# Rotary halves exchanged by ScalarE copies instead of permutation matmuls, in a six-stage transformer kernel

## The chip, the cores and the metric

One core of one Trainium2 chip. The metric is the device time of one execution of the whole program, in microseconds (us); the time of a kernel is the median of its executions. Engines are named TensorE (PE; PEld is its weight load), VectorE (DVE), ScalarE (ACT), GpSimd (POOL) and SyncE (SP).

## The reference

The program computes four layers on a sequence of 512 tokens, width 1024: an attention layer with three branches ("nsa"), a state-space layer ("s5"), and a two-layer block of an "even" mixer, a gated convolutional feed-forward, an "odd" mixer and a second feed-forward. The change touches the even mixer alone:

```python
def rope(x, pos):
    d = x.shape[-1]
    half = d // 2
    inv = ROPE_BASE ** (-jnp.arange(half, dtype=jnp.float32) / half)
    ang = pos.astype(jnp.float32)[:, None] * inv[None, :]
    cos, sin = jnp.cos(ang), jnp.sin(ang)
    xf = x.astype(jnp.float32)
    x1, x2 = xf[..., :half], xf[..., half:]
    return jnp.concatenate([x1 * cos - x2 * sin, x1 * sin + x2 * cos], axis=-1).astype(x.dtype)

def even_mixer(hn, w_in, q_gain, k_gain, ret_gain, w_out):
    s = hn.shape[1]
    p = hn @ w_in
    ...
    qa = rms_norm(to_heads(sb_q, SB_HEADS), q_gain)
    ka = rms_norm(to_heads(sb_k, SB_HEADS), k_gain)
    out_a = from_heads(stick_breaking_attention(qa, ka, to_heads(sb_v, SB_HEADS)))
    pos = jnp.arange(s)
    qb = rope(to_heads(r_q, RET_HEADS), pos)
    kb = rope(to_heads(r_k, RET_HEADS), pos)
    log_gamma = jnp.log(1.0 - jnp.exp2(-5.0 - jnp.arange(RET_HEADS, dtype=jnp.float32)))
    ret = retention_chunkwise(qb, kb, to_heads(r_v, RET_HEADS), log_gamma)
    out_b = from_heads(rms_norm(ret, ret_gain)) * jax.nn.silu(r_g)
    return jnp.concatenate([out_a, out_b], axis=-1) @ w_out
```

The retention has 4 heads of width 128. `rope` needs, beside `x`, the same tile with its two halves of 64 features exchanged and the first of them negated.

## The kernel before

Everything is held feature-major: features on the 128 partitions, the 512 tokens along the free dimension. Weights come as tiles of 128x1024 (eight chunks of 128x128) through a ring of four buffers `raw`, loaded by SyncE (L139). VectorE rounds each tile to `whi` (`split_tile`, L176), GpSimd makes the rest `wlo` (L168), and a product is three float32r matmuls a chunk: `whi` with `xh`, `whi` with `xl`, `wlo` with `xh`.

The even mixer takes 28 weight tiles, seven for each of four blocks `i`: q, k, v of two stick-breaking heads, and rq, rk, rv, rg (query, key, value, gate) of one retention head. `even_tile` numbers them and `dve_even_take` (L810) takes each finished accumulator, scaled, to an SBUF tile (`eq`, `ek`, `sq`, `rqt`, `rkt`, `rgt`). Each engine runs `stick(i)` and then `retention(i)` for `i` = 0 to 3, in an order written out by hand; the waits are semaphores, and an engine never passes an instruction that waits.

TensorE fills the gaps of this attention work with matmuls of the weight products: `beside(n)` issues `n` quarters of a weight tile (`product_beside`, L580, L581, L585; three of four quarters hold 6, 6 and 6 matmuls). In block 3 the weights of the input are through, and `beside` issues chunks of the output product instead, three matmuls each (`pe_even_out_beside`, L964, L965, L966), the first of which waits for the `wlo` of its tile.

The places that matter here, for one block:

- TensorE, end of `pe_stick`: the weighted sums of the stick-breaking heads (L715), into bank 7.
- TensorE, start of `pe_retention`: two matmuls in float32 with the permutation `swap` (L925), one of `rqt` into bank 2 and one of `rkt` into bank 3; then `beside` (3 quarters, or 3 chunks in block 3); then the four score matmuls of the retention (L930), which wait for the semaphore `r_qkv`, that is for `rqs` and `rks`; then `beside` again.
- VectorE: `rgt` taken (L810) when the tile rg is through; `eo_l` (L894), which waits for ScalarE's `eo_h`; then the bank times sine (L1007, two), and the sums `rqs`, `rks` (L1010, two). The products with cosine (L891) are made earlier.
- ScalarE, end of `act_stick`: `rvt` (L792), a table load and SiLU of `rgt` (L728), a table load back (L794), then `eo_h` from bank 7 (L796). The next that it does is the square of the retention's output (L990).

The permutation comes from the host (`host_swap`) and is loaded once at the start of `act_even` (L743). A matmul of float32 operands shows in the trace as two records with a weight load each, a float32r one as one.

Of the kernel before, what the change touches and what calls it, by code (L numbers as in the profile page):

```python
# [10 lines left out]
ACT = mybir.ActivationFunctionType  # L11
# [3 lines left out]
P = 128  # L15
# [32 lines left out]
def build(nc, A, out, names=tuple(s[0] for s in STAGES)):  # L48
# [5 lines left out]
    with ExitStack() as ctx:  # L54
# [7 lines left out]
        bank = [psum[:, b, :] for b in range(8)]  # L62
# [27 lines left out]
        def at(name, shape, dt=F32, offset=None):  # L90

            size = int(np.prod(shape[1:])) * 4
            offset = used[0] if offset is None else offset
            used[0] = offset + (size + 63) // 64 * 64
            assert used[0] <= nc.sbuf_usable_end, (name, used[0])
            return nc.alloc_sbuf_tensor_at(name, shape, dt, offset=offset)
# [398 lines left out]
        decay = etab[:, 3 * P + 2 * S:3 * P + 6 * S].rearrange("p (r s) -> p r s", r=4)  # L495
        e64eps = etab[:, 3 * P + 6 * S:3 * P + 6 * S + 1]
        egain = at("egain", [P, 3])
        swap = at("swap", [P, P])
        eq, ek, ev = (at(name, [P, S]) for name in ("eq", "ek", "ev"))
        rqt, rkt, rvt, rgt = (at(name, [P, S]) for name in ("rqt", "rkt", "rvt", "rgt"))  # L500
        qs = at("qs", [P, S])
# [11 lines left out]
        e_loaded = sem("e_loaded")  # L513
# [9 lines left out]
        e_t = sem("e_t")  # L523
# [93 lines left out]
        def even_taken(engine, name, i):  # L617

            r = even_tile(name, i)
            engine.wait_ge(acc_free[r % 2], freed(O0["even_in"] + r))  # L620
# [10 lines left out]
        def pe_head_squares(pe, i):  # L631

            if i == 0:
                pe.wait_ge(e_loaded, 48)
            for j in range(2):
                pe.wait_ge(e_sqr, 3 * i + j + 1)
                nc.tensor.matmul(bank[2 + j][:], bdiag, et[:, 2 + j, :], start=True, stop=True).then_inc(e_ms, 1)
# [102 lines left out]
        def act_even(act):  # L740
            act.dma_start(etab[:], A["even_tables"]).then_inc(e_loaded, 16)
            act.dma_start(egain[:], A["even_gains"]).then_inc(e_loaded, 16)
            act.dma_start(swap[:], A["swap"]).then_inc(e_loaded, 16)  # L743
            act.wait_ge(e_loaded, 48)
            act_head_square(act, "q", 0)
            act_head_square(act, "k", 0)
            act.preload_act_table_set(LOG_EXP)
            act_head_rstd(act, 0)
            for i in range(4):
                act_stick(act, i)  # L750
                act_retention(act, i)

        def act_stick(act, i):

            def soft(u):
                hd, jb, w = unit(u)
                act.wait_ge(e_z, 8 * i + u + 1)
                if u >= 2:
                    act.wait_ge(e_t, 8 * i + u - 1)
                if u == 1 and i:  # L760
                    act.wait_ge(r_m, i)
                nc.scalar.activation(ea[:, hd, 0:w], bank[2 + u % 3][:, 0:w], ACT.Abs).then_inc(e_abs, 1)
                act.wait_ge(e_abs, 2 * (8 * i + u) + 1)
                nc.scalar.activation(ea[:, hd, 0:w], ea[:, hd, 0:w], ACT.Exp, scale=-1.0).then_inc(e_abs, 1)
                act.wait_ge(e_abs, 2 * (8 * i + u) + 2)
                nc.scalar.activation(el[:, hd, 0:w], ea[:, hd, 0:w], ACT.Ln, bias=ones[:, 0:1]).then_inc(e_l, 1)

            def weight(u):
                hd, jb, w = unit(u)
                act.wait_ge(e_t2, 8 * i + u + 1)  # L770
                nc.scalar.activation(packed(ew, hd, jb), et[:, u % 4, 0:w], ACT.Exp).then_inc(e_w0, 1)

            soft(0)
            soft(1)
            act.wait_ge(tv_turned, TV0["even_in"] + 2 * i + 1)
            nc.scalar.activation(ev[:], bank[7][:], ACT.Copy).then_inc(tv_taken, 1)
            soft(2)
            soft(3)
            weight(0)
            weight(1)  # L780
            soft(4)
            soft(5)
            weight(2)
            weight(3)
            soft(6)
            soft(7)
            weight(4)
            weight(5)
            weight(6)
            weight(7)  # L790
            act.wait_ge(tv_turned, TV0["even_in"] + 2 * i + 2)
            nc.scalar.activation(rvt[:], bank[4][:], ACT.Copy).then_inc(tv_taken, 1)  # L792
            act_gate(act, i)
            act.preload_act_table_set(LOG_EXP)  # L794
            act.wait_ge(e_o, i + 1)
            nc.scalar.activation(eo_h[:, i, :], bank[7][:], ACT.Copy).then_inc(e_oh, 1)  # L796

# [100 lines left out]
        r_rot = sem("r_rot")  # L898
# [20 lines left out]
        def pe_retention(pe, i, beside):  # L919

            between = iter((3, 4, 2, 3) if i < 3 else (3, 3, 1, 7))
            pe.wait_ge(e_t, 8 * i + 8)
            for j in range(2):
                even_taken(pe, ("rq", "rk")[j], i)
                nc.tensor.matmul(bank[2 + j][:], swap[:], (rqt, rkt)[j][:], start=True, stop=True).then_inc(r_rot, 1)  # L925
            beside(next(between))
            pe.wait_ge(tv_taken, TV0["even_in"] + 2 * i + 2)
            pe.wait_ge(r_qkv, 2 * i + 2)
            for jb in RORDER:
                nc.tensor.matmul(retention_scores(jb), rks[:, jb * P:(jb + 1) * P], rqs[:, jb * P:S],  # L930
                                 start=True, stop=True).then_inc(r_s, 1)
            beside(next(between))
            for jb in range(4):
                pe.wait_ge(r_w, 4 * i + RORDER.index(jb) + 1)
                mm = nc.tensor.matmul(bank[6][:, jb * P:S], rvt[:, jb * P:(jb + 1) * P], packed(ew, 0, jb),
                                      start=jb == 0, stop=jb == 3)
            mm.then_inc(r_o, 1)
            beside(next(between))
            pe.wait_ge(r_sq, i + 1)
            nc.tensor.matmul(bank[5][:], ones, ea[:, 0, :], start=True, stop=True).then_inc(r_ms, 1)  # L940
            if i < 3:
                pe_head_squares(pe, i + 1)
            beside(next(between))
# [59 lines left out]
        def dve_retention(dve, i):  # L1003

            for j in range(2):
                dve.wait_ge(r_rot, 2 * i + j + 1)
                nc.vector.tensor_tensor(el[:, j, :], bank[2 + j][:], sin_t, ALU.mult).then_inc(r_part, 1)  # L1007
            for j in range(2):
                dve.wait_ge(r_part, 4 * i + 3 + j)
                nc.vector.tensor_tensor((rqs, rks)[j][:], et[:, j, :], el[:, j, :], ALU.add).then_inc(r_qkv, 1)  # L1010
            dve.wait_ge(e_o, i + 1)
            for jb in RORDER:
                dve.wait_ge(r_s, 4 * i + {0: 1, 2: 2}.get(jb, 4))
                nc.vector.tensor_tensor(packed(ew, 0, jb), retention_scores(jb), decay[:, i, 0:S - jb * P],
                                        ALU.mult).then_inc(r_w, 1)
            if i < 3:
                dve_even_take(dve, "q", i + 1)
                dve_even_take(dve, "k", i + 1)
            dve.wait_ge(r_r, i + 1)
            nc.vector.scalar_tensor_tensor(et[:, 0, :], bank[6][:], egain[:, 2:3], ea[:, 1, :],  # L1020
                                           ALU.mult, ALU.mult).then_inc(r_m, 1)
            dve.wait_ge(r_m, i + 1)
            dve.wait_ge(e_sqr, 3 * i + 3)
            nc.vector.tensor_tensor(rmix[:], et[:, 0, :], rgt[:], ALU.mult).then_inc(r_mix, 1)
            if i < 3:
                dve_head_scaled(dve, i + 1)
                dve_even_take(dve, "v", i + 1)
            for m in (2 * i, 2 * i + 1):
                nc.vector.scalar_tensor_tensor(h[:, m, :], h[:, m, :], gains[:, N_FINAL, m:m + 1], rstd[:],
                                               ALU.mult, ALU.mult).then_inc(norm_f, 1)  # L1030
            dve.wait_ge(r_hi, i + 1)
            nc.vector.tensor_tensor(eo_l[:, 4 + i, :], rmix[:], eo_h[:, 4 + i, :].bitcast(F32),
                                    ALU.subtract).then_inc(r_lo, 1)
# [1986 lines left out]
        dec.append(np.where(d >= 0, np.exp(lg * np.maximum(d, 0)) * P ** -0.5, 0.0))  # L3020
    return np.concatenate([bd, later, before, cc, sc, *dec, np.full((P, 4), 64e-6)], 1).astype(np.float32)

def host_swap():

    w = np.zeros((P, P), np.float32)
    for m in range(64):
        w[m + 64, m] = -1
        w[m, m + 64] = 1
    return w

def by_state(v):

    n = v.ndim
# [8 lines left out]
def host_arrays(I, names):  # L3042
    a = dict(weights=host_weights(I, names), tables=host_tables())
# [7 lines left out]
        cv[:, l, 3] = cols(I['ffn_conv_b_2'][l])  # L3051
    a['conv'] = cv
    a['even_tables'] = host_even_tables()
    a['swap'] = host_swap()
    q, k = I['sb_q_gain_2'][0], I['sb_k_gain_2'][0]
    a['even_gains'] = np.stack([np.concatenate([q, q]), np.concatenate([k, k]), I['ret_out_gain_2'][0]], 1)
    p, c = np.arange(P)[:, None], np.arange(S)[None, :] % P
# [46 lines left out]
```

## Time and profile before

| | |
|---|---|
| median of 3 runs | 1974.27 us (1974.04 to 1975.11) |
| the profiled execution, its own time | 1973.53 us |
| its span in the profile | 1971.7 us |
| TensorE busy | 1939.3 us, 98% |
| VectorE busy | 1141.9 us, 58% |
| ScalarE busy | 578.2 us, 29% |
| GpSimd busy | 796.2 us, 40% |
| mean granted TensorE clock | 0.995 |

The span is what the profile covers; the execution's own time is 1.8 us longer. Times inside it are counted from its start; the even mixer runs from about 710 to 965 us. The granted clock is given as a share of 2.4 GHz; 0.5 is 1.2 GHz. Busy time of TensorE is the union of its records, whose ends are modelled: two records that overlap do not run at the same time.

### The profile page before, as it was taken

The numbers are of one execution on the slowest core, as the hardware profiler recorded it, in microseconds if no ns is written. First come the engines' busy times: TensorE is split into PE (matmuls) and PEld (weight loads), VectorE is DVE, ScalarE is ACT, GpSimd is POOL, SyncE is SP. The second block draws the span as 40 slices with busy tenths as digits, with TensorE's granted clock in tenths as the row PEclk, the third lists the DMA queues.
The fourth block names the chain that finished last, engine by engine and source line by source line (L and its number), as shares of the span: only waits on it lengthen the run. The fifth ranks groups of instructions, "written<-read, shape, count | busy, mean of one in ns | idle before, by whom it ended". The sixth has DMA issues, their size and how long they took to land.

```text
span 1971.7 us, 26522 instructions
## 1 busy us (share of the span) xinstructions
PE 1939.3 (98%) x9866; PEld 1516.7 (77%) x9866; DVE 1141.9 (58%) x2077; ACT 578.2 (29%) x1118; POOL 796.2 (40%) x454
## 2 busy tenths in 40 slices
PE   8999999999999999999999999999999999999999
PEld 5967777777878776777778888886788878888887
DVE  5779998787974545676654545333554454445311
ACT  3135566316630134454221111101332221111000
POOL 3632231367854332222334444443233334444443
PEclk9999999999999999999999999999999999999999
DMA  5611110223122231111233222232112222222232
GB/s 184 189 67 37 40 33 33 86 86 97 44 66 95 89 120 54 65 65 54 65 108 99 96 96 96 96 107 86 65 64 75 75 88 97 98 99 98 98 119 73
DMA packets 54021, 167.66 MB, mean 85 GB/s; under 512 B 6801, under 2 KB 14865, under 8 KB 53537
## 3 DMA queue, kind: packets, MB, share of 16 engines
q1 hardware_dynamic: 46624, 155.21, 23.9%
q10 hardware_dynamic: 7296, 11.09, 2.0%
q8 instruction: 65, 1.06, 0.2%
q14 instruction: 36, 0.29, 0.0%
HBM read 157.90 MB, written 2.10 MB: 81 GB/s over the span
## 4 chain that ended last, share of the span: by engine, by line
PE 90%; DVE 7%; issue 1%; ACT 1%; DMA 0%; ACTq 0%; POOL 0%; DVEq 0%
PE bank L185 18%; PE bank L189 18%; PE bank L186 18%; PE bank L580 5%; PE bank L585 5%; PE bank L581 5%; DVE prob L1649 2%; DVE ssb L1636 2%; PE bank L1271 1%; PE bank L201 1%; PE bank L1296 1%; PE bank L204 1%; PE bank L2607 1%; PE bank L198 1%; PE bank L2618 1%
## 5 line engine op out<-in xcount | busy, mean ns | idle before, releaser
L168 POOL TENSOR_TENSOR wlo<-raw,whi 128x1024 fp32r<-128x1024 f32 x248 | 595.7, 2402 | 921.5 <-DVE whi L176 921.5
L176 DVE CAST whi<-raw 128x1024 fp32r<-128x1024 f32 x288 | 205.5, 714 | 361.3 <-PE bank L189 255.2
L185 PE MATMUL bank<-xh,whi 128*128 128x512 f32 x888 | 347.9, 392 | 0.0
L186 PE MATMUL bank<-xl,whi 128*128 128x512 f32 x888 | 346.3, 390 | 0.0
L189 PE MATMUL bank<-xh,wlo 128*128 128x512 f32 x888 | 219.3, 389 | 0.0
L185 PEld LDWEIGHTS bank<-xh,whi 128*128 128x128 f32 x888 | 167.2, 188 | 38.6 <-issue 3.9
L186 PEld LDWEIGHTS bank<-xl,whi 128*128 128x128 f32 x888 | 167.2, 188 | 35.1 <-issue 0.5
L189 PEld LDWEIGHTS bank<-xh,wlo 128*128 128x128 f32 x888 | 166.7, 188 | 34.6
L580 PE MATMUL bank<-xh,whi 128*128 128x512 f32 x424 | 175.3, 414 | 0.0
L581 PE MATMUL bank<-xl,whi 128*128 128x512 f32 x424 | 165.9, 391 | 0.0
L185 PE MATMUL bank<-ghi,whi 128*128 128x512 f32 x308 | 122.6, 398 | 0.0
L186 PE MATMUL bank<-glo,whi 128*128 128x512 f32 x308 | 120.7, 392 | 0.0
L1697 POOL TENSOR_TENSOR wlo<-raw,whi 128x1024 fp32r<-128x1024 f32 x22 | 52.0, 2365 | 151.7 <-DVE whi L176 151.7
L585 PE MATMUL bank<-xh,wlo 128*128 128x512 f32 x424 | 109.1, 394 | 0.0
L580 PEld LDWEIGHTS bank<-xh,whi 128*128 128x128 f32 x424 | 79.7, 188 | 24.5 <-issue 8.1
L585 PEld LDWEIGHTS bank<-xh,wlo 128*128 128x128 f32 x424 | 78.8, 188 | 18.7 <-issue 2.0
L581 PEld LDWEIGHTS bank<-xl,whi 128*128 128x128 f32 x424 | 79.8, 188 | 16.6 <-issue 2.2
L1649 DVE TENSOR_SCALAR prob<-prob,gsig,stat 128x128 f32<-128x128 f32 (+3 forms) x128 | 89.3, 739 | 2.3
L459 DVE TENSOR_TENSOR upad<-bank,rstd 128x512 f32<-128x512 f32 x44 | 30.5, 693 | 103.1 <-PE bank L189 91.8
L472 DVE TENSOR_TENSOR bank<-bank,rstd 128x512 f32<-128x512 f32 x44 | 30.8, 699 | 100.7 <-PE bank L189 100.7
L440 ACT ACTIVATE bank<-upad,cw 128x512 f32<-128x512 f32 x44 | 34.4, 782 | 156.9 <-DVE upad L459 156.9
L189 PE MATMUL bank<-ghi,wlo 128*128 128x512 f32 x308 | 78.7, 395 | 0.0
(427 smaller groups left out, 3480.6 us busy)
## 6 DMA issues: line engine op xcount, KB each, us to landing
raw<-in_weights_dram SPq DMA_DIRECT2D x288, 512.0 KB, 3.3
h<-in_x_dram SPq DMA_DIRECT2D x2, 1024.0 KB, 7.0
out_dram<-h ACTq DMA_DIRECT2D x4, 512.0 KB, 2.6
etab<-in_even_tables_dram ACTq DMA_DIRECT2D x1, 1730.0 KB, 6.5
sz<-su SPq DMA_DIRECT2D x16, 64.0 KB, 2.0
sz<-su SPq DMA_DIRECT2D x16, 48.0 KB, 2.0
x_kh<-kvc_h ACTq DMA_DIRECT2D x2, 256.0 KB, 5.1
x_kl<-kvc_l ACTq DMA_DIRECT2D x2, 256.0 KB, 7.0
```

The lines of the kernel that those rows point to most:

```text
L168: nc.gpsimd.tensor_tensor(wlo[:, s % 2, :], raw[:, s, :], whi[:, s % 2, :].bitcast(F32), ALU.subtract).then_inc(w_lo, 1)
L176: nc.vector.tensor_copy(whi[:, t_of_4 % 2, :], raw[:, t_of_4, :]).then_inc(w_hi, 1)
L185: nc.tensor.matmul(to, w_h[k], rhs_hi(k), start=first and k == 0, stop=False)
L186: nc.tensor.matmul(to, w_h[k], rhs_lo(k), start=False, stop=False)
L189: last_mm = nc.tensor.matmul(to, w_l[k], rhs_hi(k), start=False, stop=last and k == chunks - 1)
L440: nc.scalar.activation(c0, upad[:, 2:], ACT.Identity, bias=cw[:, layer, 3, f:f + 1], scale=cw[:, layer, 2, f:f + 1]).then_inc(u_copied, 1)
L580: nc.tensor.matmul(to[:], w_h, xh[:, k, :], start=k == 0, stop=False)
L581: nc.tensor.matmul(to[:], w_h, xl[:, k, :], start=False, stop=False)
L585: mm = nc.tensor.matmul(to[:], wlo[:, par, k * P:(k + 1) * P], xh[:, k, :], start=False, stop=k == KC - 1)
L1636: nc.vector.tensor_tensor_reduce(ssb[:, br, hd, 0:w], bank[2 + c][:, 0:w], dist[:, i % 2, hd, (3 - qb) * P:S], -1.0, 3e38, ALU.add, ALU.mi ...
L1649: mul = nc.vector.tensor_scalar(prob[:, br, hd, 0:w], prob[:, br, hd, 0:w], gsig[:, qb, g:g + 1], stat[:, 8 + 2 * br + hd:9 + 2 * br + hd] ...
L1697: nc.gpsimd.tensor_tensor(wlo[:, r % 2, :], raw[:, r % 4, :], whi[:, r % 2, :].bitcast(F32), ALU.subtract).then_inc(w_lo, 1)
```

## The change

The two permutation matmuls of each block go, with their wait, the tile `swap`, its load and its host array. In their place ScalarE makes four copies a block, each of 64 partitions by 512: from the upper half of the partitions of `rqt` (then `rkt`) to the lower half of bank 2 (then 3), with scale -1.0, and from the lower to the upper half, with scale 1.0. They stand in `act_stick` after the table load that follows SiLU and ahead of `eo_h`. VectorE's wait counts two copies for each of its multiplies.

```diff
@@ pe_head_squares @@
-                pe.wait_ge(e_loaded, 48)
+                pe.wait_ge(e_loaded, 32)
@@ act_even @@
-            act.dma_start(swap[:], A["swap"]).then_inc(e_loaded, 16)
-            act.wait_ge(e_loaded, 48)
+            act.wait_ge(e_loaded, 32)
@@ new function @@
+        def act_halves(act, i):
+
+            act.wait_ge(e_t, 8 * i + 8)
+            for j in range(2):
+                even_taken(act, ("rq", "rk")[j], i)
+                for half in range(2):
+                    there, here = slice(64 * half, 64 * half + 64), slice(64 - 64 * half, 128 - 64 * half)
+                    nc.scalar.activation(bank[2 + j][there, :], (rqt, rkt)[j][here, :], ACT.Copy,
+                                         scale=1.0 if half else -1.0).then_inc(r_rot, 1)
@@ act_stick @@
             act_gate(act, i)
             act.preload_act_table_set(LOG_EXP)
+            act_halves(act, i)
             act.wait_ge(e_o, i + 1)
             nc.scalar.activation(eo_h[:, i, :], bank[7][:], ACT.Copy).then_inc(e_oh, 1)
@@ pe_retention @@
-            pe.wait_ge(e_t, 8 * i + 8)
-            for j in range(2):
-                even_taken(pe, ("rq", "rk")[j], i)
-                nc.tensor.matmul(bank[2 + j][:], swap[:], (rqt, rkt)[j][:], start=True, stop=True).then_inc(r_rot, 1)
             beside(next(between))
@@ dve_retention @@
-                dve.wait_ge(r_rot, 2 * i + j + 1)
+                dve.wait_ge(r_rot, 4 * i + 2 * j + 2)
                 nc.vector.tensor_tensor(el[:, j, :], bank[2 + j][:], sin_t, ALU.mult).then_inc(r_part, 1)
```

ScalarE's order at the end of block 0's stick-breaking part, before (`rgt` is the gate, `eo_h` the rounded output of the two heads; in brackets the semaphores that an instruction waits for):

```order
L792 ACTIVATE rvt<-bank 128x512 [waits tv_turned]
L728 ACT_TABLE_LOAD
L728 ACTIVATE rgt<-rgt 128x512 [waits acc_free0]
L794 ACT_TABLE_LOAD
L796 ACTIVATE eo_h<-bank 128x512 [waits e_o]
L990 ACTIVATE ea<-bank 128x512 [waits r_o]
```

and with the change (its line numbers differ by a few):

```order
L800 ACTIVATE rvt<-bank 128x512 [waits tv_turned]
L727 ACT_TABLE_LOAD
L727 ACTIVATE rgt<-rgt 128x512 [waits acc_free0]
L802 ACT_TABLE_LOAD
L758 ACTIVATE bank<-rqt 64x512 [waits acc_free1,e_t]
L758 ACTIVATE bank<-rqt 64x512
L758 ACTIVATE bank<-rkt 64x512 [waits acc_free0]
L758 ACTIVATE bank<-rkt 64x512
L805 ACTIVATE eo_h<-bank 128x512 [waits e_o]
L995 ACTIVATE ea<-bank 128x512 [waits r_o]
```

Four copies stand between the table load and `eo_h`, behind SiLU and both table loads.

TensorE's order in block 3, before, from the end of the weighted sums to the score matmuls:

```order
L715 MATMUL bank<-ew,ev 64x128 x2
L925 MATMUL bank<-rqt,swap 128x512 [waits acc_free0,e_t]
L925 MATMUL bank<-rkt,swap 128x512 [waits acc_free1]
L964 MATMUL bank<-eo_h,whi 128x512 [waits acc_free0,w_lo]
...
L930 MATMUL bank<-rqs,rks 128x512 [waits r_qkv,tv_taken]
```

With the change the two rows of L925 are gone there and in the three other blocks, and nothing else on TensorE moves. VectorE's order is the same; in it `eo_l` stands ahead of the multiplies by sine, which `rqs` and `rks` need (block 0, before):

```order
L810 TENSOR_TENSOR rgt<-bank,xf 128x512
L894 TENSOR_TENSOR eo_l<-bank,eo_h 128x512 [waits e_oh]
L1007 TENSOR_TENSOR el<-bank,etab 128x512 [waits r_rot] x2
L1010 TENSOR_TENSOR rqs<-et,el 128x512 [waits r_part]
L1010 TENSOR_TENSOR rks<-et,el 128x512 [waits r_part]
```

## Rows read from the trace of the kernel before

**Rows 1.** The page, busy time of the engines, and the chain by engine

```profile
PE 1939.3 (98%) x9866; PEld 1516.7 (77%) x9866; DVE 1141.9 (58%) x2077; ACT 578.2 (29%) x1118; POOL 796.2 (40%) x454
...
PE 90%; DVE 7%; issue 1%; ACT 1%; DMA 0%; ACTq 0%; POOL 0%; DVEq 0%
```

**Rows 2.** Waits of PE, whole span: us in total, times, longest

```profile
PE bank L1119 <- DVE wgate L1509: 5.9, 1, 5.9
PE bank L1258 <- DVE cpr L1622: 4.8, 8, 3.0
...
PE bank L930 <- DVE rks L1010: 0.8, 1, 0.8
```

**Rows 3.** Timeline of block 1: start us, us, engine, line, what [idle before]

```profile
819.71 2.38 PE L715 MATMUL bank<-ew,ev 128*64 128x512 f32 x16
...
820.42 0.68 DVE L810 TENSOR_TENSOR rgt<-bank,xf 128x512 f32<-128x512 f32 x1
...
821.14 0.63 ACT L728 ACTIVATE rgt<-rgt 128x512 f32<-128x512 f32 x1 [2.72 <-DVE rgt L810]
...
821.79 1.28 ACT L794 ACT_TABLE_LOAD   x1
...
822.01 1.13 PE L925 MATMUL bank<-rqt,swap 128*128 128x512 f32 x2
...
822.97 1.02 PE L925 MATMUL bank<-rkt,swap 128*128 128x512 f32 x2
...
823.08 0.60 ACT L796 ACTIVATE eo_h<-bank 128x512 fp32r<-128x512 f32 x1
...
823.43 0.79 PE L580 MATMUL bank<-xh,whi 128*128 128x512 f32 x1
823.71 0.69 DVE L894 TENSOR_TENSOR eo_l<-bank,eo_h 128x512 fp32r<-128x512 f32 x1 [2.60 <-ACT eo_h L796]
...
826.11 0.68 DVE L1010 TENSOR_TENSOR rks<-et,el 128x512 f32<-128x512 f32 x1
...
827.73 0.41 PEld L930 LDWEIGHTS bank<-rqs,rks 128*128 128x128 f32 x2
...
830.00 1.00 PEld L585 LDWEIGHTS bank<-xh,wlo 128*128 128x128 f32 x5
```

**Rows 4.** Line L1010 over the span: xcount, ns min/median/max, first and last start

```profile
L1010 DVE TENSOR_TENSOR rks<-et,el x4: 681/682/683, 765.0 to 948.3; 128x512 f32<-128x512 f32 x4
```

**Rows 5.** Timeline of block 3

```profile
942.81 2.35 POOL L168 TENSOR_TENSOR wlo<-raw,whi 128x1024 fp32r<-128x1024 f32 x1 [4.18 <-DVE whi L176]
...
947.92 0.40 PE L966 MATMUL bank<-eo_h,wlo 128*128 128x512 f32 x1
948.34 0.68 DVE L1010 TENSOR_TENSOR rks<-et,el 128x512 f32<-128x512 f32 x1
949.13 0.30 PEld L930 LDWEIGHTS bank<-rqs,rks 128*128 128x128 f32 x2 [1.25 <-issue]
...
951.29 0.19 PEld L964 LDWEIGHTS bank<-eo_h,whi 128*128 128x128 f32 x1
```

**Rows 6.** ScalarE groups by shape: busy us, mean ns | idle before

```profile
L247 ACT ACTIVATE bank<-h 128x512 f32<-128x512 f32 x36 | 21.6, 601 | 182.8 <-DVE h L378 153.0 <-DVE h L2824 26.1 <-DVE ssq L260 3.6
...
L1453 ACT ACTIVATE cpt<-bank 64x512 f32<-64x512 f32 x8 | 4.7, 591 | 3.0 <-PE bank L1258 3.0
```

**Rows 7.** Timeline of ScalarE, a write into a bank and its successor

```profile
697.72 0.60 ACT L247 ACTIVATE bank<-h 128x512 f32<-128x512 f32 x1 [4.35 <-DVE h L2824]
698.25 0.71 ACT L2796 ACTIVATE xh<-h,seedt 128x512 fp32r<-128x512 f32 x1
```

**Rows 8.** Timeline of PE at the wait of 3.0 us

```profile
133.53 1.06 PE L1258 MATMUL bank<-tables,cpr 128*64 128x128 f32 x4 [3.04 <-DVE cpr L1622]
```

**Rows 9.** Windows there: busy by engine, granted clock, DMA share, GB/s

```profile
130.00:131.00 1.00, 0.49 (x8) 0.30 (x6) 0.93 (x4) 0.00 (x0) 1.00 (x2) 0.86 0.29 37
...
137.00:138.00 1.00, 1.00 (x6) 0.81 (x5) 0.95 (x6) 0.51 (x2) 0.00 (x0) 0.72 0.00 0
```

More of the change, by code:

```diff
@@ L497, in build @@
         egain = at("egain", [P, 3])
-        swap = at("swap", [P, P])
         eq, ek, ev = (at(name, [P, S]) for name in ("eq", "ek", "ev"))
@@ L3021, in host_even_tables @@
     return np.concatenate([bd, later, before, cc, sc, *dec, np.full((P, 4), 64e-6)], 1).astype(np.float32)
[L3023 to L3029, printed above, removed]
 def by_state(v):
@@ L3053, in host_arrays @@
     a['even_tables'] = host_even_tables()
-    a['swap'] = host_swap()
     q, k = I['sb_q_gain_2'][0], I['sb_k_gain_2'][0]
```

## The prediction

> **What bounds the kernel now.** I read the page first: TensorE is busy for 98% of the span and makes 90% of the chain that ended last [rows 1]. So time is what TensorE must do plus what it waits, and I went to its waits. They are few: the two longest lie in the first 140 us (5.9 and 3.0 us), and in the even mixer the score matmuls L930 waited once, 0.8 us, for `rks` [rows 2]. That is the place where the change works, so the third view is the timeline of the end of one block [rows 3], and then of block 3, whose filler work differs [rows 5].
>
> The reader is to see two things in block 1 [rows 3]. TensorE ends the weighted sums L715 at 822.09, does the permutations, and reaches L930 at 827.73, while `rks` is ready at 826.11 + 0.68 = 826.79: TensorE has 0.94 us of margin, and no more. And the chain that makes `rks` runs over ScalarE already: `rgt` taken until 821.10, SiLU to 821.77, table load to 823.07, `eo_h` 823.08, `eo_l` 823.71, two multiplies by sine, two sums. ScalarE and VectorE pass it on without a pause; it was the table loads and `eo_h`, not the permutation matmuls, that set when VectorE came to the sines. There are four such blocks [rows 4]; blocks 0 and 2 read like block 1, with TensorE's margin the same. In block 3 `rks` ends at 949.02 and L930's load follows at 949.13: margin nil, and that is the wait of 0.8 us.
>
> **What is removed.** Two matmuls a block, two records each. From the start of L925 at 822.01 to that of L580 at 823.43 are 1.4 us [rows 3]; L580's 0.79 us, twice what its successors show, says that it queued behind them for some 0.4 us more. So TensorE gets 1.4 to 1.8 us a block, 5.7 to 7.2 us in all, **if nothing waits instead**. In block 3 part of it is lost at once: the first output chunk waits for `wlo`, which GpSimd ends at 942.81 + 2.35 = 945.16 [rows 5].
>
> The load of `swap` and its share of a wait go too. ScalarE's first squares may start a little sooner; TensorE has no wait there among [rows 2], so I cost it at nothing. If the squares did come sooner, `qs` and `ks` would only wait longer for TensorE.
>
> **What is added.** Four copies a block on ScalarE, of 64 partitions by 512, into a bank. The trace has no such copy from half to half, so I bound it. A ScalarE write of 128x512 into a bank takes 601 ns, and its successor started 0.53 us after it [rows 6, 7]. An instruction on 64 partitions is no cheaper: 591 ns for 64x512 [rows 6]. I take 0.53 us each, 2.12 us a block; the upper end is 0.60 (no overlap), 2.40 us; the lower end, against that row, is half of 0.53, if a half tile were half a tile: 1.06 us.
>
> Where they stand decides. They are behind SiLU and both table loads and ahead of `eo_h`, which shows no wait for its own matmuls (it started when the table load ended). So `eo_h` moves by the full 2.12 us; `eo_l` waits for it, and the sines, `rqs` and `rks` are queued behind `eo_l` on VectorE. The banks are full by then, so `r_rot` is never the last wait. `rks` comes 2.12 us later, and L930 waits for `rks`.
>
> **The sum.** From the end of `rks` to the load after the four scores, where TensorE waited for nothing else, are 951.29 - 949.02 = 2.27 us [rows 5].
> - Block 1: `rks` ends at 826.79 + 2.12 = 828.91, and the load after the scores follows at 831.18, against 830.00 before [rows 3]: **+1.18 us**. Blocks 0 and 2 the same: 3 x 1.18 = 3.54 us.
> - Block 3: no margin, so the whole **+2.12 us**.
> - Together **+5.66 us**, all in TensorE's waits. What the permutations gave back becomes stall as well: TensorE would come to L930 at 827.73 - 1.4 to 1.8 and can start at 829.02, an idle time of 2.7 to 3.1 us; in block 3 it ends its chunks some 0.5 to 0.9 us earlier than 948.32 and starts at 951.25, an idle time of 3.4 to 3.9 us.
>
> After L930 everything hangs on TensorE again, so nothing is given back. ScalarE's next work after `eo_h` comes only with the retention's output, far behind; VectorE's next waits are for TensorE's scores.
>
> **The clock** is the second term. The trace shows that idle time can cost it: before the wait of 3.04 us TensorE ran sparse small matmuls, and the granted clock of 0.86 in 130 to 131 us means that it fell to 0.5 (1.2 GHz) at 130.72, at the start of the wait. It came back in the window 137 to 138 (0.72, so at 137.56), though TensorE had worked again since 133.53 [rows 8, 9]. That is 4.0 us of work at half clock: **2.0 us lost for one fall**. The wait of 0.8 us before L930 cost nothing of the kind. The new stalls of 2.7 to 3.9 us lie between, amid dense work and not behind sparse work, so each can bring a fall or not, and that may differ from one execution to the next. I take two of the four: +4.0 us. The bounds are none (0) and all four (+8.0).
>
> The Trainium skill, "TensorE: Matmul & The Clock Gate", section "Why this matters for your kernels", speaks against this change: it asks for no long idle gaps between bursts of matmuls, since one brings TensorE back to the lower clock. The trace agrees that it falls around a wait of 3.04 us; by the rule the longest stall alone would pay, which is the second case below.
>
> The sum is made on the profiled execution: 1973.53 + 5.66 + 4.0 = 1983.2. It lies 0.74 us below the median of the runs, so for the median: 1974.27 + 9.66 = **1983.9 us**, 0.5% slower.
>
> **The rivals**, each with its time:
> - *Stalls, two falls of the clock* (forecast): 1983.9. Chance 0.33.
> - *Stalls, one fall*, after block 3, whose stall is the longest and the only one above 3.1 us: 1974.27 + 5.66 + 2.0 = 1981.9. For it: the one fall in the middle of the program came with a stall of just over 3 us. Chance 0.20.
> - *Stalls, no fall*: 1979.9. For it: TensorE works densely on both sides of the new stalls, unlike at 130 us. Chance 0.18.
> - *Stalls, three or four falls*: 1985.9 to 1987.9. For it: the stalls of blocks 0 to 2 differ from 3.04 us by little. Chance 0.17.
> - *Not slower*: a copy on half of the partitions costs half, 0.265 us. Then `rks` moves by 1.06 us, which the margin of 0.94 all but covers: 3 x 0.12 + 1.06 = 1.42 us, 1975.7, with stalls shorter by 1.06 us and no fall. In general the sum is 16 copies less 3 x 0.94; it stays under 3.9 us while a copy is below 0.42 us. Against it: 591 ns for 64x512. Chance 0.09.
> - *Faster*: the copies hide and TensorE keeps the 5.7 to 7.2 us: 1967.1 to 1968.6. That asks for copies that run ahead of SiLU, when `rkt` is long there and ScalarE idles 2.72 us [rows 3]; the order has them behind it, and ScalarE passes nothing that waits. It would also take the change not doing what the order shows. Chance 0.03.
>
> **How the numbers follow.** 0.2% is 3.9 us, about what a measurement of this kernel can tell from no change. The cases of stalls lie all beyond it, 0.88 together; the cheap copy is "same", 0.09; faster 0.03. The range takes in the four cases of stalls but for their edges: from 1979.0 (no fall, copies 0.06 us cheaper than taken) to 1988.0 (four falls). Copies at 0.60 us would add 16 x 0.07 = 1.1 us to each case.
>
> **What would show it.** In the profile of the changed kernel: L925 gone; 16 copies of 64x512 at about 0.59 us, 0.53 apart; `eo_h` 2.1 us later behind SiLU; TensorE's wait for `rks` at the scores four times, 2.7 to 3.1 us and once 3.4 to 3.9, some 12 us in all against 0.8; the interval from one block to the next 62.3 us instead of 61.1; the clock at 0.5 for a few us behind some of these stalls, and the mean clock a little under 0.995. I am wrong if the copies are shorter than 0.42 us, if the wait for `rks` does not appear in blocks 0 to 2, or if the clock falls after none or all of the stalls.

## The result, and the profile after

The changed kernel takes 1985.15 us (median of 5 runs, 1984.7 to 1985.52); the kernel before, in the same comparison, 1974.19 us. The ratio is 1.0057, 95% interval 1.0046 to 1.0068: 0.6% slower. The prediction was 1983.9 us, range 1979.0 to 1988.0.

First the page of the changed kernel, busy time and chain:

```profile
span 1983.4 us, 26505 instructions
...
PE 1939.4 (98%) x9850; PEld 1517.2 (76%) x9850; DVE 1142.5 (58%) x2077; ACT 587.6 (30%) x1134; POOL 796.9 (40%) x454
...
PE 88%; DVE 8%; ACT 2%; issue 1%; DMA 0%; ACTq 0%; POOL 0%; DVEq 0%
```

TensorE has 16 records less than in [rows 1], yet the same busy time, and the span is 11.7 us longer. TensorE's share of the chain fell by two points and those of ScalarE and VectorE rose by one each. TensorE's waits (us in total, times, longest) name the place; the scores are now line L935:

```profile
PE bank L935 <- DVE rks L1015: 13.8, 4, 4.9
PE bank L1263 <- DVE cpr L1627: 4.7, 8, 2.9
PE bank L1124 <- DVE wgate L1514: 4.7, 1, 4.7
```

The wait for `rks` was 0.8 us, once [rows 2]; it is 13.8 us, four times. The timeline of block 1 shows how it comes about:

```profile
822.26 2.38 PE L714 MATMUL bank<-ew,ev 128*64 128x512 f32 x16
...
823.69 0.63 ACT L727 ACTIVATE rgt<-rgt 128x512 f32<-128x512 f32 x1 [2.72 <-DVE rgt L819]
...
824.34 1.28 ACT L802 ACT_TABLE_LOAD   x1
825.63 1.22 ACT L758 ACTIVATE bank<-rqt 64x512 f32<-64x512 f32 x2
826.88 1.22 ACT L758 ACTIVATE bank<-rkt 64x512 f32<-64x512 f32 x2
828.03 0.58 ACT L805 ACTIVATE eo_h<-bank 128x512 fp32r<-128x512 f32 x1
...
828.64 0.69 DVE L903 TENSOR_TENSOR eo_l<-bank,eo_h 128x512 fp32r<-128x512 f32 x1 [4.99 <-ACT eo_h L805]
829.25 1.28 DVE L1012 TENSOR_TENSOR el<-bank,etab 128x512 f32<-128x512 f32 x2
...
831.04 0.68 DVE L1015 TENSOR_TENSOR rks<-et,el 128x512 f32<-128x512 f32 x1
831.84 0.30 PEld L935 LDWEIGHTS bank<-rqs,rks 128*128 128x128 f32 x2 [3.33 <-issue]
831.87 3.36 PE L935 MATMUL bank<-rqs,rks 128*128 128x512 f32 x8 [2.94 <-DVE rks L1015]
```

From the end of the table load `eo_h` was at once [rows 3]; now the four copies stand between, 825.63 to 828.03: 2.40 us, 0.60 us each. VectorE idled 4.99 us for `eo_h`, where it had idled 2.60. And TensorE idled 2.94 us, then ran the scores in 3.36 us; in block 3 of the kernel before they took 2.39. The windows show why (busy time by engine, then the granted clock, 0.83 in the first row, DMA share and GB/s):

```profile
765.00:770.00 5.00, 2.36 (x5) 1.45 (x6) 3.24 (x7) 0.00 (x0) 0.00 (x0) 0.83 0.01 3
770.00:775.00 5.00, 5.00 (x20) 3.77 (x20) 2.42 (x5) 0.00 (x0) 1.09 (x1) 0.83 0.00 0
830.00:835.00 5.00, 3.13 (x9) 1.96 (x9) 2.75 (x5) 0.00 (x0) 0.00 (x0) 0.81 0.01 3
...
895.00:900.00 5.00, 3.90 (x16) 2.85 (x17) 2.82 (x7) 0.00 (x0) 0.00 (x0) 1.00 0.00 0
955.00:960.00 5.00, 1.36 (x2) 0.84 (x3) 3.09 (x5) 0.37 (x1) 0.00 (x0) 0.60 0.03 13
960.00:965.00 5.00, 5.00 (x16) 3.38 (x15) 1.87 (x4) 0.00 (x0) 0.00 (x0) 0.71 0.00 0
```

The clock fell to 1.2 GHz around the stalls of blocks 0, 1 and 3, and not around that of block 2, which was 2.94 us as well. Windows of 1 us place the first two falls more exactly, block 0 and then block 1:

```profile
768.00:769.00 1.00, 1.00 (x3) 0.34 (x2) 0.00 (x0) 0.00 (x0) 0.00 (x0) 0.65 0.07 16
...
833.00:834.00 1.00, 1.00 (x4) 0.59 (x3) 0.92 (x2) 0.00 (x0) 0.00 (x0) 0.57 0.00 0
```

In both, the window before still has 1.00, so the clock fell at 768.3 and 833.1, 0.7 and 1.3 us after TensorE had started the scores again (767.64 and 831.87). In block 3 it fell at 956.0, inside the stall. These are the falls of the one execution that was profiled; the mean clock of all five was 0.991 or 0.992.

Block by block the 11.7 us are found. I take the starts of the weighted sums (L715, now L714) and, for block 3, the time from there to the product with `rvt` (L935, now L940), all read from the timelines:

| from | before, us | after, us | difference |
|---|---|---|---|
| block 0 to 1 | 61.12 | 64.24 | 3.12 |
| block 1 to 2 | 61.11 | 64.22 | 3.11 |
| block 2 to 3 | 61.11 | 62.54 | 1.43 |
| block 3, L715 to L935 | 11.56 | 16.03 | 4.47 |

That is 12.13 us; what stands ahead of the weighted sums of block 0 was 0.57 us shorter in this execution (758.02 against 758.59) and its rest 0.14 longer. Block 2 shows the chain without a fall of the clock: +1.43. Blocks 0 and 1 show 1.7 us more.

### The profile page after: what moved, and what is told of

Read it like the earlier page. It is cut to its first block, busy times and chain, and to the rows that moved or that the text cites. A ratio compares the mean times of both kernels' runs of the same rounds, so it can differ in the third digit from the quotient of the medians.

```text
span 1983.4 us, 26505 instructions
## 1 busy us (share of the span) xinstructions
PE 1939.4 (98%) x9850; PEld 1517.2 (76%) x9850; DVE 1142.5 (58%) x2077; ACT 587.6 (30%) x1134; POOL 796.9 (40%) x454
## 4 chain that ended last, share of the span: by engine, by line
PE 88%; DVE 8%; ACT 2%; issue 1%; DMA 0%; ACTq 0%; POOL 0%; DVEq 0%
PE bank L185 18%; PE bank L186 17%; PE bank L189 17%; PE bank L584 5%; PE bank L579 5%; PE bank L580 4%; DVE prob L1654 2%; DVE ssb L1641 2%; PE bank L1276 1%; PE bank L201 1%; PE bank L1301 1%; PE bank L204 1%; PE bank L2612 1%; PE bank L198 1%; PE bank L2623 1%
```

## The experiments

All are edits of the changed kernel; the two that run the permutation matmuls keep the load of `swap` too. Counts of falls and block times are those of the one profiled execution of each kernel. The kernel before had a median of 1973.86 us beside the first four runs, 1973.91 beside the next three and 1974.0 beside the last two.

**The permutation matmuls kept, for nothing.** Their results go to banks that nobody reads; the copies feed the sines.

```diff
             between = iter((3, 4, 2, 3) if i < 3 else (3, 3, 1, 7))
+            pe.wait_ge(e_t, 8 * i + 8)
+            for j in range(2):
+                even_taken(pe, ("rq", "rk")[j], i)
+                nc.tensor.matmul(bank[5 + j][:], swap[:], (rqt, rkt)[j][:], start=True, stop=True)
             beside(next(between))
```

> The changed kernel with the permutation matmuls put back on TensorE, their results written to banks 5 and 6 and used by nobody: the copies feed the sines as in the change. Theory (the added chain of four ScalarE copies sets the scores, and idle time costs the clock): the chain is the same, so TensorE's four waits for rks shrink by the 1.4 to 1.8 us of matmuls that fill them (about 1.3 us each in blocks 0 to 2), rks comes no later than with the change, and the clock no longer falls in blocks 0 and 1: 1.44 us a block for three blocks and 2.4 for the fourth over the kernel before, so 1981 us, or 1983 if the clock still falls in block 3. The kernel gets faster by 2 to 4 us although TensorE does more. Rival (the copies alone make up the time, the clock is a by-product, or TensorE has no time to spare there): same as the change or slower, 1985 to 1992 us.

Measured: 1980.64 us (5 runs, ratio 1.0036, interval 1.0022 to 1.0049), 4.5 us **less** than the change, with more work on TensorE. In the block times it is 3.8 us less (203.27 us against 207.03 for the four rows of the table above). Its waits and its windows:

```profile
PE bank L941 <- DVE rks L1021: 6.9, 4, 3.2
```

```profile
765.00:770.00 5.00, 3.79 (x16) 2.54 (x15) 3.32 (x6) 0.29 (x1) 0.00 (x0) 1.00 0.02 4
...
830.00:835.00 5.00, 3.88 (x16) 2.81 (x17) 2.81 (x7) 0.00 (x0) 0.00 (x0) 1.00 0.00 0
...
955.00:960.00 5.00, 3.75 (x10) 2.47 (x11) 2.37 (x5) 0.00 (x0) 0.00 (x0) 0.74 0.00 0
```

Stalls of 1.2 us in blocks 0 to 2 leave the clock alone; the one of 3.2 us in block 3 brings a fall. The three block intervals are 62.56, 62.57 and 62.57 us: the chain costs 1.45 us a block, and the difference to 64.23, 1.67 us, is what one fall cost. The stall itself cost nothing beyond the chain: filled or not, `rks` came at the same time behind the weighted sums. That the median fits the expected 1981 us is partly luck: for a fall left in block 3 the expectation had 1983, the block times give 1973.86 + 8.4 = 1982.2, and the rest comes for the most part from a stretch of low clock elsewhere in the program that was shorter in this run; the next run is about it.

**The same, and block 3 filled too**, by the two matmuls once more ahead of its scores:

```diff
             beside(next(between))
+            for j in range(2 if i == 3 else 0):
+                nc.tensor.matmul(bank[5 + j][:], swap[:], (rqt, rkt)[j][:], start=True, stop=True)
```

> The run with the permutation matmuls kept beside the copies, and in block 3 the same two matmuls once more, ahead of the scores, their results unused: the last stall of more than 3 us, 3.2 us in that run, is filled to 1.5 us. Theory (idle time costs the clock, one fall was left in block 3 and cost some 1.6 us): no fall in the even mixer any more, and block 3 is back to its chain alone: 1979.0 us, faster than the run with less work by 1.6 us. Rival (the low clock in block 3 comes from something other than TensorE's idle time): 1980.6 us or, with the added work exposed, up to 1982.4.

Measured: 1980.52 us (6 runs), no less than the run before it. In the even mixer the expectation held: longest wait 1.5 us, the clock 1.00 throughout, and block 3 took 13.94 us from L715 to its product with `rvt`, against 15.57: 1.63 us less. So what low clock block 3 had came from TensorE's idle time. The profile shows where the 1.63 us went. The odd mixer has a stretch of low clock of its own, around 1390 us. In this run:

```profile
1385.00:1390.00 5.00, 3.93 (x11) 1.89 (x10) 2.50 (x4) 2.67 (x5) 1.95 (x1) 0.86 0.00 0
1390.00:1395.00 5.00, 5.00 (x9) 2.16 (x8) 4.27 (x7) 4.05 (x7) 0.40 (x1) 0.50 0.32 107
1395.00:1400.00 5.00, 5.00 (x16) 3.92 (x15) 2.25 (x3) 2.90 (x5) 0.00 (x0) 0.61 0.00 0
```

and in the one with the matmuls kept:

```profile
1390.00:1395.00 5.00, 4.45 (x10) 2.13 (x11) 3.50 (x6) 2.34 (x4) 2.35 (x1) 0.93 0.11 20
1395.00:1400.00 5.00, 5.00 (x18) 3.92 (x18) 4.90 (x7) 4.61 (x9) 0.00 (x0) 0.73 0.23 89
```

(1 - clock) x 5 us x 2 gives the time at 1.2 GHz: 10.3 us here, 3.4 us there, and 6.8 us in the kernel before (its rows stand further down; the window after them has 0.98). From the product with `rvt` to the end of the span are 1020.05, 1016.69 and 1018.2 us: the rest of the program moves by 1.5 to 1.9 us up or down with the length of that stretch. The part ahead of the even mixer moves too: the weighted sums of block 0 start at 757.29 in this run and at 758.94 in the one before, and the low clock near 130 us lasts 3.4 us here and 6.8 us there. So the medians alone could not decide this pair; the block times do. Why the stretch is shorter or longer was not tried.

**The removal alone.** No copies and no wait for them; the sines multiply what the banks hold, so the rotation is left out.

```diff
             act.preload_act_table_set(LOG_EXP)
-            act_halves(act, i)
...
-                dve.wait_ge(r_rot, 4 * i + 2 * j + 2)
```

> The changed kernel without the copies and without the wait for them: the multiplies by sine read what the banks hold, so the rotation is left out. This is what the removal is worth alone. Theory: rks is where it was in the kernel before, margin 0.94 us in three blocks and none in the fourth, so only 0.8 to 0.9 us a block come back: 1971.7 us, and the waits for rks are some 0.7 us in three blocks. Rival (TensorE's 1.4 to 1.8 us a block come back whole): 1967.1 to 1968.6 us.

Measured: 1971.78 us (11 runs, ratio 0.9990, interval 0.9981 to 0.9999). Block intervals 60.18, 60.19 and 60.18 us: 0.93 us a block, the margin, and not the 1.7 us of the matmuls. The waits for `rks` are 4.3 us in total, 2.6 at the longest. That one, in block 3, brought a fall of the clock:

```profile
945.00:950.00 5.00, 3.73 (x7) 2.11 (x8) 2.24 (x4) 0.00 (x0) 0.00 (x0) 0.66 0.03 12
```

Block 3 takes 13.22 us instead of 11.56: with this fall the removal alone makes it 1.66 us longer.

**The copies ahead of SiLU**, their place the only change:

```diff
+            act_halves(act, i)
             act_gate(act, i)
             act.preload_act_table_set(LOG_EXP)
-            act_halves(act, i)
```

> The copies ahead of SiLU and its table load instead of behind both. Theory: ScalarE idles 2.7 us there in blocks 1 to 3 (1.4 in block 0), so the copies are hidden and eo_h starts where it did before the change, in block 0 about 1.0 us later: about 0 in block 0, -0.9 us in blocks 1 and 2, 0 in block 3, no fall of the clock in the even mixer: 1972.4 us. Rival (VectorE or the bank writes are disturbed by the copies, or the copies themselves are what costs wherever they stand): 1980 us or more.

Measured: 1971.14 us (11 runs, ratio 0.9989, interval 0.9980 to 0.9998). The intervals, 61.28, 60.18 and 60.19 us, are +0.16 for block 0 and -0.93 for blocks 1 and 2, as with no copies at all. The copies are hidden in ScalarE's idle time. The 13.8 us of waits become 5.4. The stall of block 3 is 2.57 us, as in the run before, but the clock stayed at 1.00 and the block took 11.57 us: between these two runs one fall alone cost 1.65 us.

**Only VectorE's order changed**, copies where the change has them:

```diff
             split("F")
+            for j in range(2):
+                dve.wait_ge(r_rot, 4 * i + 2 * j + 2)
+                nc.vector.tensor_tensor(el[:, j, :], bank[2 + j][:], sin_t, ALU.mult).then_inc(r_part, 1)
+            for j in range(2):
+                dve.wait_ge(r_part, 4 * i + 3 + j)
+                nc.vector.tensor_tensor((rqs, rks)[j][:], et[:, j, :], el[:, j, :], ALU.add).then_inc(r_qkv, 1)
             dve.wait_ge(e_oh, i + 1)
```

(and taken away at the head of `dve_retention`)

> The change with its copies where they are, behind SiLU; only VectorE's order is changed: the multiplies by sine and the sums stand ahead of eo_l. Theory (the copies cost because eo_h and eo_l are queued behind them and the sines behind eo_l): the sines start with the copies, the second one at the end of the fourth, and rks is ready about 0.5 us later than in the kernel before instead of 2.4. TensorE then comes to the scores 0.2 to 0.4 us earlier a block than in the kernel before, and in block 3 0.6 us later: 1973 to 1974 us, the waits for rks near 1.5 us, no fall of the clock in blocks 0 to 2. Rival (the copies are the cost, wherever their readers are queued): 1980 us or more.

Measured: 1973.67 us (11 runs, ratio 0.9999, interval 0.9990 to 1.0008), the time of the kernel before. VectorE in block 1:

```profile
824.26 0.69 DVE L904 TENSOR_TENSOR el<-bank,etab 128x512 f32<-128x512 f32 x1 [3.23 <-ACT bank L758]
825.50 0.69 DVE L904 TENSOR_TENSOR el<-bank,etab 128x512 f32<-128x512 f32 x1 [0.55 <-ACT bank L758]
...
826.71 0.69 DVE L907 TENSOR_TENSOR rks<-et,el 128x512 f32<-128x512 f32 x1
827.31 0.68 DVE L909 TENSOR_TENSOR eo_l<-bank,eo_h 128x512 fp32r<-128x512 f32 x1
```

The sines overlap the copies now, and `rks` ends 6.33 us after the start of SiLU (821.07), against 8.03 with the change and 5.65 before. The same four copies in the same place cost 11 us behind one order of VectorE and nothing measurable behind the other. The block intervals are 60.85 us; one fall remained, in block 3, at a stall of 3.2 us. By the block times the even mixer is 1.5 us longer than before (3 x -0.26 and 13.86 against 11.56 us in block 3), and the odd mixer's stretch of low clock lasted 3.4 us instead of 6.8: that the median comes out even is in part this.

**Both edits together**: copies ahead of SiLU, sines and sums ahead of `eo_l`.

> As the run with the copies ahead of SiLU, and on VectorE the two multiplies by sine and the two sums moved ahead of eo_l, right behind the taking of rgt. Theory: rks is then ready at about 2.5 us behind rgt, well ahead of TensorE, so no wait for rks is left and TensorE keeps what the permutations took: 1.4 to 1.8 us in each of three blocks, and in block 3 the 0.85 us of its old wait and some 0.8 more: 1967 to 1968.5 us, faster than both kernels. Rival (something else holds the scores, such as the waits of the score matmuls on rvt, or VectorE gets too late for its next split): 1971 us or more, with a new wait in TensorE's list.

Measured: **1964.34 us** (5 runs, 1963.5 to 1965.72; ratio 0.9952, interval 0.9939 to 0.9966), faster than the kernel before by 0.5% and than the change by 1.0%. TensorE waits nowhere for `rks`. Block 1 in its timeline:

```profile
817.96 2.37 PE L714 MATMUL bank<-ew,ev 128*64 128x512 f32 x16
...
819.27 1.28 DVE L904 TENSOR_TENSOR el<-bank,etab 128x512 f32<-128x512 f32 x2
819.39 0.63 ACT L727 ACTIVATE rgt<-rgt 128x512 f32<-128x512 f32 x1 [0.24 <-DVE rgt L819]
...
821.70 0.68 DVE L907 TENSOR_TENSOR rks<-et,el 128x512 f32<-128x512 f32 x1
...
824.25 0.41 PEld L941 LDWEIGHTS bank<-rqs,rks 128*128 128x128 f32 x2
```

`rks` is ready at 822.38, 1.87 us before TensorE's load. The intervals are 59.38 us three times, 1.73 us a block below the 61.11 of the kernel before: the permutation matmuls come back whole, and block 3 takes 8.88 us instead of 11.56. Together that is 7.9 us, which is the difference of the profiled spans (1963.8 against 1971.7); the medians differ by 9.5. The remaining 1.6 us are of the size by which the stretch of low clock in the odd mixer moves a run; that it was this was not shown.

**What a copy costs.** Two whole copies instead of four halves (the exchange, and so the rotation, left out):

```diff
-                for half in range(2):
...
-                    nc.scalar.activation(bank[2 + j][there, :], (rqt, rkt)[j][here, :], ACT.Copy,
-                                         scale=1.0 if half else -1.0).then_inc(r_rot, 1)
+                nc.scalar.activation(bank[2 + j][:], (rqt, rkt)[j][:], ACT.Copy,
+                                     scale=-1.0).then_inc(r_rot, 2)
```

> Two copies of 128 partitions instead of four of 64, same place; the halves are not exchanged, so the rotation is left out. Theory (a copy costs by its free size, not by its partitions, 0.60 us each in a row): the chain is 1.2 us longer than in the kernel before instead of 2.4, 0.25 us a block in blocks 0 to 2 and 1.2 in block 3: 1976 us, 1978 if the clock falls once. Rival (half a tile is half the cost, so two whole copies cost what four halves do): as the change, 1985 us.

Measured: 1975.71 us (10 runs, ratio 1.0010, interval 1.0000 to 1.0019). A whole copy took 584 to 602 ns where half a one takes 596; but the two stand 0.53 us apart, the overlap that I had taken for the change:

```profile
822.78 0.60 ACT L756 ACTIVATE bank<-rqt 128x512 f32<-128x512 f32 x1
823.31 0.58 ACT L756 ACTIVATE bank<-rkt 128x512 f32<-128x512 f32 x1
823.84 0.58 ACT L803 ACTIVATE eo_h<-bank 128x512 fp32r<-128x512 f32 x1
```

The block intervals are 61.24 us, 0.13 above the kernel before: two copies of 0.53 us less the margin of 0.94. Block 3 took 15.47 us, 3.91 more, for its stall of 3.6 us brought a fall:

```profile
945.00:950.00 5.00, 1.55 (x7) 0.94 (x5) 3.08 (x5) 1.88 (x4) 0.14 (x1) 0.92 0.34 105
950.00:955.00 5.00, 4.84 (x10) 2.97 (x11) 1.32 (x4) 0.00 (x0) 0.00 (x0) 0.50 0.00 0
955.00:960.00 5.00, 5.00 (x20) 3.63 (x18) 0.56 (x2) 0.30 (x1) 0.00 (x0) 0.89 0.00 0
```

Less the two copies that is 2.85 us for a low clock of 6.9 us. So the median, which fits the expectation without a fall (1976 us), fits by luck: the odd mixer's stretch was short in this run, 3.4 us instead of 6.8, and the copies were cheaper than expected.

**Four half copies that stay on their partitions** (the exchange left out):

```diff
-there, here = slice(64 * half, 64 * half + 64), slice(64 - 64 * half, 128 - 64 * half)
+there, here = slice(64 * half, 64 * half + 64), slice(64 * half, 64 * half + 64)
```

> The change with each copy going to the partitions it comes from: the exchange is left out, all else is equal. Theory (0.60 us a copy in a row is what writes into a bank take): spacing and time as in the change, 1985 us. Rival (crossing the partitions costs the 0.07 us by which the copies exceeded the 0.53 us that I had taken): 0.53 us apart, the chain 0.28 us shorter a block, 1984 us.

Measured: 1984.47 us (4 runs, ratio 1.0054, interval 1.0039 to 1.0070), block intervals 64.24, 64.21 and 62.56 us: the change over again, with a pair of copies in 1.22 us. The medians could not tell the two expectations apart, 1 us from each other with runs from 1983.87 to 1986.19; the block times and the copies do. Crossing the partitions costs nothing that shows here.

**The banks in turn**: lower half of bank 2, lower half of bank 3, then the upper halves.

```diff
+            for half in range(2):
+                there, here = slice(64 * half, 64 * half + 64), slice(64 - 64 * half, 128 - 64 * half)
+                for j in range(2):
...
-                dve.wait_ge(r_rot, 4 * i + 2 * j + 2)
+                dve.wait_ge(r_rot, 4 * i + j + 3)
```

> The change with its four copies in another order: lower half of bank 2, lower half of bank 3, then the upper halves, so that no copy follows one into the same bank. Two whole copies into two banks stood 0.53 us apart, four half copies 0.62. Theory A (a copy waits for the one before it where both write the same bank): all are 0.53 us apart, the chain is 0.3 us shorter a block, 16 x 0.08 less for the sum: 1984 us. Theory B (a copy of 64 partitions never overlaps its neighbour): 0.62 us apart, 1985 us as the change.

Measured: 1983.53 us (4 runs, ratio 1.0050, interval 1.0034 to 1.0066). ScalarE in block 0:

```profile
761.27 0.59 ACT L759 ACTIVATE bank<-rqt 64x512 f32<-64x512 f32 x1
761.81 0.58 ACT L759 ACTIVATE bank<-rkt 64x512 f32<-64x512 f32 x1
762.41 0.60 ACT L759 ACTIVATE bank<-rqt 64x512 f32<-64x512 f32 x1
762.95 0.58 ACT L759 ACTIVATE bank<-rkt 64x512 f32<-64x512 f32 x1
763.47 0.58 ACT L806 ACTIVATE eo_h<-bank 128x512 fp32r<-128x512 f32 x1
```

Neither theory held. The starts are 0.54, 0.60, 0.54 and 0.52 us apart: the wide gap is where the copies change from one half of the partitions to the other; within one half they overlap. The bank changes at each of the first three steps, so it is not the bank. The scale changes at the wide gap too, but in the run with two whole copies it changed from -1.0 to 1.0 between the second copy and `eo_h`, 0.53 us apart. Whether the half that is read or the half that is written counts was not separated. In the change every copy follows one on the other half. The chain is 0.2 us a block shorter than with the change (block 1 to 2, without a fall, 62.36 us). The falls of the clock were three again, but in blocks 0, 2 and 3.

## Why the prediction came out right

**The chain, step by step, held.** Copies behind both table loads; `eo_h`, `eo_l`, sines and sums queued behind them; the margin of 0.94 us used up; everything on TensorE's waits. The removal alone gave 0.93 us a block (taken: the margin of 0.94), the copies ahead of SiLU cost nothing, and the reordering of VectorE alone took `rks` from 8.03 to 6.33 us behind SiLU's start and the intervals to 60.85 us. These are three separate tests of the same chain.

**The price of a copy was too low**: 0.53 us taken, 0.60 measured as the mean of a row of four. I read the overlap from a pair in which a write of 128 partitions was followed by another such instruction [rows 7]; for halves in alternation it doesn't hold. The term was +5.66 us; it measured 3 x 1.45 + 2.38 = 6.73 us (block intervals with the matmuls kept, and block 3 of the filled run, 13.94 against 11.56). The upper end that I gave, 0.60 without overlap, was the measured value. That half a tile is no cheaper (596 ns) was right, and with it the end of the rival "not slower".

**The falls of the clock were three, not two.** Prices: 1.67 us in blocks 0 and 1, and 4.47 - 2.38 = 2.1 us in block 3, against 2.0 taken: 5.4 us in all where I had 4.0. So the time is that of the case "three or four falls", to which I gave 0.17. It asked for 1985.9 us at least; 0.75 us less was measured. The price was near, though the stretches were not what I had read at 130 us: in blocks 0 and 1 the clock was low for 3.4 us, all of it work, and half of that is 1.7 us; in block 3 it was low for 6.9 us, from 956.0, and TensorE worked in 4.2 us of them, half of which is 2.1 us. The Trainium skill, "TensorE: Matmul & The Clock Gate", section "Why this matters for your kernels", asks for no long idle gaps between bursts of matmuls. The case that I had drawn from it, in which the longest stall alone pays, did not come: stalls of 2.94 us paid too, in two blocks of three.

The test of this term is the run in which TensorE does more and the program takes 4.5 us less, 3.8 of them in the even mixer. Its rival, that the copies alone make up the time, asked for 1985 us or more.

**What was luck.** The range, 1979.0 to 1988.0, held every number of falls from none to four, so that the result lies in it speaks for the chain and says next to nothing of the clock; that two of four stalls would bring a fall was a guess with no row behind it, and it was missed. In the block times the change costs 12.13 us where I had 9.66, 2.47 more. The median came only 1.25 us above the forecast, because the rest of the program was 0.43 us shorter in the profiled execution and the profiled execution of the kernel before was 0.74 us faster than the median to which I added.

**Two readings of mine were wrong**, without harm to the number. First, I wrote that the kernel before has one fall of the clock in the middle of the program. It has another, in the odd mixer:

```profile
1380.00:1385.00 5.00, 3.93 (x10) 1.74 (x9) 2.63 (x4) 2.91 (x5) 2.35 (x1) 0.84 0.01 3
1385.00:1390.00 5.00, 5.00 (x9) 2.50 (x9) 4.70 (x7) 4.05 (x8) 0.00 (x0) 0.50 0.29 105
```

Windows over the whole span would have shown it, and it is the one whose length differed from kernel to kernel and moved the time of an execution by 1.5 to 1.9 us. Second, in block 3 I let the first output chunk wait for the tile that GpSimd ended at 945.16 [rows 5]. With the change the chunk started at 951.33, while the corresponding tile ran from 949.90 to 952.28: it is that of the next tile. So TensorE kept all 1.7 us of the permutation there, and its stall was 4.9 us, not 3.4 to 3.9. A longer stall ahead of the same `rks` changes no end.

**The stalls.** 2.7 to 3.1 us were forecast for blocks 0 to 2 and 2.94 came; about 12 us in all, and 13.8 came, the difference being block 3 and the dearer copies. For the interval I wrote 62.3 us; block 2, the one without a fall, shows 62.5. Both come with the 0.07 us a copy.

## What to carry to other kernels

Work taken off the busiest engine pays only where that engine does not then wait: read the margin between its arrival and the last operand, here 0.94 us, before counting what is removed. Where substitute work goes on another engine is worth more than its amount: the same four copies cost 11 us behind SiLU and nothing ahead of it, and an unrelated instruction (`eo_l`) queued between them and their reader made up 1.7 us of the 2.4 by which `rks` came later. Idle time of TensorE can have a second price, the clock. In this kernel stalls of 1.2 to 1.7 us brought no fall, stalls of 2.6 to 2.9 us some, and those of 3.2 us and more in the even mixer each brought one; so cost such a stall at what the operand comes later, plus 1.6 to 2.9 us for each fall that it may bring. And where a stretch of low clock elsewhere moves the whole time by nearly 2 us, read a small effect from the times inside the program, not from the medians.

## What was unexpected of the hardware

- More matmuls made the program faster: +1.7 us of TensorE work a block, results unused, and 4.5 us less, of which 3.8 lie in the even mixer and the rest outside it.
- Equal stalls did not bring equal falls: of three stalls of 2.94 us the first and second brought one in the change, the first and third with the banks in turn (there 2.73 to 2.74 us). A stall of 2.6 us in block 3 brought one in the run with the removal alone and none in the run with the copies first. What decides it was not settled.
- After a fall the low clock lasted for 3.4 to 10.3 us, for the most part with TensorE at work, and one and the same place in the odd mixer showed 3.4, 6.8 and 10.3 us in different kernels.
- Successive ScalarE copies into banks overlap by some 0.06 us when they stay on the same partitions (starts 0.53 to 0.54 us apart) and not when they change between the lower and the upper 64 (0.60 to 0.62 us).
